# Four pads in SBUF that shift the stationary tiles against the weight ring, modulo 256 bytes

## The reference

```python
h = x
h = h + gated_deltanet(rms_norm(h, g0), ...)          # 32 heads of 128, chunks of 64
h = h + (silu(n @ w_gate) * (n @ w_up)) @ w_down      # n = rms_norm(h), hidden 5632
shared = nsa_shared_kv(h, ...)                        # K/V projections, compressed blocks
h = h + nsa_attention(rms_norm(h, g1), shared, ...)   # 16 heads, 4 groups
h = h + (silu(n @ w_gate) * (n @ w_up)) @ w_down
return rms_norm(h, g_final)
```

## Time and profile before

| what | us |
|---|---|
| three runs | 2800.06, 2800.52, 2799.73 |
| their median | 2800.06 |
| the profiled execution's own time | 2803.94 |
| its span, first to last instruction | 2802.1 |
| TensorE busy, matmuls | 2739.6 |
| TensorE busy, weight loads | 2282.1 |
| VectorE busy | 2219.6 |
| ScalarE busy | 1648.4 |
| GpSimd busy | 31.0 |

### The profile page before, as it was taken

The page is one execution under the profiler, slowest core; times in us unless marked ns, Lnnn a source line. Parts: engine busy times, 40 slices in busy tenths (PEclk is TensorE's granted clock), DMA queues, the critical chain, the costliest instruction groups (busy, mean ns, idle before and its releaser), DMA issues.

```text
span 2802.1 us, 40252 instructions
## 1 busy us (share of the span) xinstructions
PE 2739.6 (98%) x13456; PEld 2282.1 (81%) x13456; DVE 2219.6 (79%) x2727; ACT 1648.4 (59%) x2184; POOL 31.0 (1%) x30
## 2 busy tenths in 40 slices
PE   8999999999988999999999999999999999999998
PEld 6878888888877888888888888888887888888887
DVE  5867877878767788888888876557677888888887
ACT  6766767667665555555555555554555555555554
POOL 0000000000000000000000000000000000000000
PEclk9999999999999999999999999999999999999999
DMA  6534444445433566656666656643345666656664
GB/s 239 181 124 153 159 144 163 156 149 167 158 105 113 166 210 199 198 185 203 198 198 203 198 172 224 222 135 114 106 158 188 207 199 200 199 184 200 198 201 166
DMA packets 135097, 493.23 MB, mean 176 GB/s; under 512 B 15009, under 2 KB 15329, under 8 KB 134625
## 3 DMA queue, kind: packets, MB, share of 16 engines
q1 hardware_dynamic: 133776, 487.82, 52.8%
q10 hardware_dynamic: 1232, 4.23, 0.4%
HBM read 489.86 MB, written 2.13 MB: 176 GB/s over the span
## 4 chain that ended last, share of the span: by engine, by line
PE 65%; issue 29%; DVE 3%; ACT 2%; DMA 1%; POOL 0%; POOLq 0%; DVEq 0%; SPq 0%; ACTq 0%
PE ACC L733 10%; PE ACC L735 10%; PE ACC L734 10%; PE SIDE L943 7%; PE SIDE L944 7%; PE SIDE L945 7%; PE ACC L943 3%; PE ACC L944 3%; PE ACC L945 3%; PE SIDE L741 2%; DVE W_LO L1627 1%; DMA RAW<-stream 1%; PE SIDE L1138 1%; ACT W_HI L1194 0%; ACT WORK L1587 0%
## 5 line engine op out<-in xcount | busy, mean ns | idle before, releaser
L1627 DVE TENSOR_TENSOR W_LO<-RAW,W_HI 128x1024 fp32r<-128x1024 f32 x424 | 511.6, 1222 | 268.9 <-ACT W_HI L1194 265.8
L1194 ACT ACTIVATE W_HI<-RAW 128x1024 fp32r<-128x1024 f32 x424 | 443.3, 1057 | 217.5 <-PE ACC L735 183.8
L1436 ACT ACTIVATE W_HI<-WORK 128x1024 fp32r<-128x1024 f32 x320 | 325.4, 1031 | 345.8 <-PE SIDE L945 232.7
L733 PE MATMUL ACC<-W_HI,X_HI 128*128 128x512 f32 x1216 | 491.2, 404 | 17.7 <-DVE W_LO L1627 17.6
L735 PE MATMUL ACC<-W_HI,X_LO 128*128 128x512 f32 x1216 | 477.6, 393 | 0.0
L734 PE MATMUL ACC<-W_LO,X_HI 128*128 128x512 f32 x1216 | 476.7, 392 | 0.0
L1878 DVE TENSOR_TENSOR W_LO<-WORK,W_HI 128x1024 fp32r<-128x1024 f32 x300 | 364.5, 1221 | 119.0 <-ACT W_HI L1436 116.3
L1436 ACT ACTIVATE W_HI<-RAW 128x1024 fp32r<-128x1024 f32 x328 | 314.8, 980 | 237.0 <-PE ACC L735 141.6
L733 PE MATMUL ACC<-W_HI,A_HI 128*128 128x512 f32 x928 | 370.3, 399 | 0.7 <-issue 0.7
L735 PE MATMUL ACC<-W_HI,A_LO 128*128 128x512 f32 x928 | 362.7, 391 | 0.0
L734 PE MATMUL ACC<-W_LO,A_HI 128*128 128x512 f32 x928 | 362.2, 390 | 0.0
(11 more groups left out here) (363 smaller groups left out, 3798.7 us busy)
## 6 DMA issues: line engine op xcount, KB each, us to landing
RAW<-stream SPq DMA_DIRECT2D x752, 512.0 KB, 4.6
WORK<-stream SPq DMA_DIRECT2D x160, 512.0 KB, 4.8
WORK<-gdn_rows ACTq DMA_DIRECT2D x8, 512.0 KB, 6.2
WORK<-xt SPq DMA_DIRECT2D x4, 512.0 KB, 9.3
H<-x SPq DMA_DIRECT2D x2, 1024.0 KB, 13.6
out<-WORK SPq DMA_DIRECT2D x4, 512.0 KB, 3.5
WORK<-tails SPq DMA_DIRECT2D x2, 512.0 KB, 10.8
WORK<-gfin SPq DMA_DIRECT2D x1, 1024.0 KB, 6.6
```

The source lines that it names most:

```text
L733: nc.tensor.matmul(dst, hi[:, at:at + P], wh, start=first and h % 2 == 0 and q == 0, stop=False)
L1194: nc.scalar.activation(W_HI[:, h % WS, :], raw_piece(h), ACT.Copy).then_inc(hi_ready, 1)
L1436: nc.scalar.activation(dst, src, ACT.Copy).then_inc(hi_ready, 1)
L1627: nc.vector.tensor_tensor(W_LO[:, h % WS, :], raw_piece(h), W_HI[:, h % WS, :].bitcast(f32), SUB).then_inc(lo_ready, 1)
```

## The change

Four tensors are declared between the others: GAP_X of 16 float32 columns (64 bytes in each partition) ahead of X_HI, GAP_A of 56 (224 bytes) ahead of A_HI, GAP_B of 16 (64 bytes) ahead of B_HI, and GAP_Z of 24 (96 bytes) ahead of TR. No instruction names them. All that is declared behind a pad moves up by its size.

```diff
         RAW = sb("RAW", [P, RAWS, PIECE])
         W_HI, W_LO = (sb(n, [P, WS, PIECE], f32r) for n in ("W_HI", "W_LO"))
+        sb("GAP_X", [P, 16])
         X_HI, X_LO = (sb(n, [P, KT * SEQ], f32r) for n in ("X_HI", "X_LO"))
-        A_HI, A_LO, B_HI, B_LO = (sb(n, [P, CHK * SEQ], f32r) for n in ("A_HI", "A_LO", "B_HI", "B_LO"))
+        sb("GAP_A", [P, 56])
+        A_HI, A_LO = (sb(n, [P, CHK * SEQ], f32r) for n in ("A_HI", "A_LO"))
+        sb("GAP_B", [P, 16])
+        B_HI, B_LO = (sb(n, [P, CHK * SEQ], f32r) for n in ("B_HI", "B_LO"))
         H = sb("H", [P, NT, DM])
+        sb("GAP_Z", [P, 24])
         TR, UR, NR, YQ, YB = (sb(n, [P, 1024], f32r) for n in ("TR", "UR", "NR", "YQ", "YB"))
```

## The result

The changed kernel takes 2850.33 us (median of 4 runs, 2849.58 to 2855.09), the kernel before beside it 2800.29 (4 runs, 2799.73 to 2801.63). The ratio is 1.0182 [1.0164, 1.0199]: **50 us slower**, where 2790 was forecast and the range ended at 2830. The profiled execution took 2850.04 us, with a granted clock of 0.998. Lines moved by 5, so L733 to L735 are now L738 to L740, and L943 to L945 are L948 to L950.

What follows compares the result with a forecast made beforehand. TensorE's stream bounds the kernel: 10,512 ring matmuls 226.7 ns apart, 2383 us, 85% of the span. Taking 10.5 us off 2803.94 gives 2793.4, off the median 2800.06 gives 2789.6; forecast 2790 us, range 2735 to 2830.

Steps and rivals of the forecast that it cites:

- What a distance costs: Ring matmuls: stationary loads 64 bytes off take 1 ns less on each of 10,512, −10.5 us.
- the upper end: Largest gain on the ring matmuls, 5 ns each, −53 us, from records before transposes, 392 against 397 ns.
- a settled rhythm is lost: FFN loop and GDN: switches between unlike distances disturb the 226.7 ns step; +6 to +46 us, given as 2823; chance 0.28.
- addresses do nothing: Ring matmuls: independent reads would not care about 64 bytes; 2800 us; chance 0.22, including gains and losses that cancel.
- A lower rhythm: Ring matmuls settle 6.67 ns lower, at 220.0: X alone 2758, all families 2730; range 2672 to 2770, chance 0.21.
- its far end: From L840's plain float32 products, read as two passes each: 12.2 ns less per ring matmul, −128 us, 2672; 3 in 100.
- The isolated gap of 216 ns: Skill's figure for 512 columns, N / 2.4 + 2.5; by it the sum would be 2688.
- The argument against the slow side from the compression: Compression's products, stationary slices at changing distances, average 118 ns, no worse than settled rows; set against the lost rhythm.
- transfers into WORK cost nothing: FFN: two of six transfer slots lie in WORK, landing in 4.8 us against 4.6; no cost.
- VectorE and ScalarE stayed covered: FFN: shifted operands bounded at 10% either way on 36 us, covered by VectorE's slack, costed at 0.
- the spread in L944's records: Sign of the lost rhythm in the FFN: minimum and maximum 385 and 398, where now 389 and 393, median 389.
- The point from which that rival decides: FFN loop: a mean spacing above 227.3 ns decides for the lost rhythm.

Runs made afterwards that it cites:

- e2: Against the kernel before, one 64-byte pad ahead of X_HI, all stationary tiles alike at distance 64 from the ring: 2855.7 us, ratio 1.0203.
- e7: Against the kernel before, one pad ahead of X_HI puts all stationary tiles at distance 192 from the ring: 2817.1 us, ratio 1.0070.
- e8: Against the kernel before, only W_LO moved, 64 bytes off; W_HI and all stationary tiles stay at distance 0: 2842.49 us, ratio 1.0159.
- e1: Against the kernel before, only X moved, to 64 bytes from the ring; A, B, Z, H and WORK stay at 0: 2834.20 us, ratio 1.0125.
- e13: Kernel before with ring products loading 32 of 128 stationary columns and writing 32 of 128 output rows, distance 0: 2835.17 us, ratio 1.0131.
- e14: Kernel before with loads of 32 of 128 stationary columns, 32 output rows, and 16 columns of pad ahead of X_HI: 2834.00 us, ratio 1.0127.
- e12: Against the kernel before, ring begins 16 bytes into one tensor, all stationary tiles at distance 240: 2840.8 us, ratio 1.0146.
- e9: Against the kernel before, one pad ahead of X_HI puts all stationary tiles at distance 224 from the ring: 2856.6 us, ratio 1.0204.
- e3: Against the kernel before, one 256-byte pad ahead of X_HI, distance again 0 modulo 256: 2799.7 us, ratio 1.0002.

## Why the prediction was wrong

**The step that failed is "What a distance costs".** It took 1 ns off each of the 10,512 matmuls, from a record of 388 beside a load at 64 bytes against 389 beside one at 0, and at best 5 ns off, from 392 against 397. Measured at a distance of 64: 6.6 ns more (233.3 against 226.7, e2). Sign and size were wrong. Each of those rows is one matmul with one odd load beside it. Four of the five start out of a settled stream. The 392 doesn't: the five intervals before it are 236, 228, 233, 230 and 227 ns, so the 5 ns that were to be the upper end compare two states of the stream and not two distances. Such a single row shows what happens next to a rhythm that still stands, not what the stream does when every load is like that: in e7 a third of the FFN's X records read 388 while the kernel is 19 us slower. I had also bounded the cost from one side only. Both rows gave a gain, and I let the price of the unsettled state stand as a rival's where it was the other end of the same unknown.

**The rival "a settled rhythm is lost" came out**, near its fullest size: 4.4 ns on every matmul, 2846 us, against 5.5 and 2850. Its number came from the earlier trace rows, five starts at 232 ns after a small step; set against 226.7 these would have been 5.3 ns and 2856. It was the one row shown in which a whole stretch ran unsettled, and it was within 1 ns of the 232.9 that the changed kernel averages. That it came so near is in part luck, because the mechanism was wrong. I had distances that are unlike break the rhythm at each change, in the FFN loop, and so halved the price to 2823. e2 has all alike and is the slower for it: none of the other eight distances settles at 226.7 at all. Alternation adds its part (e8, and Z in e1), but A alone runs at 233.3 in the changed kernel.

**Rivals that fell.** That addresses do nothing is refuted by e2 alone. The Trainium skill, "TensorE: Matmul & The Clock Gate", "Part 2: What happens when you issue a matmul", says that TensorE has two independent read ports, so that loading the next weights takes no read bandwidth from the running matmul. The runs don't agree with it as a rule about time: the same reads in the same number cost 226.7 or 233.3 ns by the distance of their addresses. That a shorter load gives nothing back at distance 0 (e13) fits it; that it gives 1.7 ns back at 64 (e14 against e2) doesn't. A lower rhythm was found for no distance with 512 columns, and its multiples of 16 cycles (6.67 ns) don't hold either: 228.8 ns (e7, settled) and 231.6 (e12) are none. The row for its far end was misread, which touches no sum: L840 runs two float32 products with two records each, not four. The isolated gap of 216 ns that the Trainium skill has on the same page ("Back-to-back issue gap") was not reached either; the lowest steady step of any run here is 226.7. The argument against the slow side from the compression (118 ns at changing distances) was of 256 moving columns, and the gate product and e9 show that these don't carry over to 512.

**What held.** TensorE's stream is the time: one nanosecond on each interval under 260 is 10 us, and 5.46 ns gave +54.5 of it. The bytes of the pads and the distances hold, as the families' different means show. Counts, forms and waits did not change, transfers into WORK cost nothing, and VectorE and ScalarE stayed covered: the wait on W_LO fell from 17.6 to 14.2 us, which fits a slower TensorE that gives VectorE more time. Of the signs I named, the spread in L944's records came, but with the median gone from 389 to 394 too: it was a new step, not a disturbed old one. The point from which that rival decides, a mean of 227.3 ns in the FFN loop, was passed by 5.4.

## What to carry to other kernels

Where TensorE's stream is the bound and each matmul has its own weight load, the layout in SBUF is part of the schedule. For float32r products of 512 moving columns, keep stationary and moving tiles at the same address modulo 256 bytes (with 256 columns the gate product gained at 224), and after any edit that shifts a tensor by less than that, read some twenty starts in a row before anything else. The change in the mean of all short intervals, times their count, gives the change in time to a few us (e2: 5.9 × 9,988 = 59 us for 57). The settled interval alone says too much (6.6 × 10,512 = 69), since the old stream isn't settled everywhere. Don't price a steady stream from one instruction at its edge; take the row in which a whole stretch ran that way, even if it comes from another stage.

## What the runs showed that I had not expected

- 64 bytes that nobody reads, ahead of X_HI, make this kernel 2.0% slower (e2), and 256 bytes make no difference (e3: 1.0002).
- The patterns repeat to 1 ns. A run at 96 bytes goes 234 235 234 231 238 237 231 ns over and over. At 64 bytes some runs go 233 233 234 and others 231 236, with one mean.
- A weight load of a quarter of the length goes with a slower stream, a mean of 231.6 ns against 227.4 (e13).
- 256 moving columns can go below their settled 120.0 ns: 116.7 at a distance of 224, where 512 columns go up to 233.3.
- None of the 14 kernels beat the one before; its layout with everything at distance 0 is the best of the nine distances tried. Distances that aren't multiples of 32 bytes were tried once (e12), and other pairs of unlike distances for W_HI and W_LO only in e8.
